# Attention with the values as the stationary operand: what the chip makes of a reordered softmax normalisation

## The reference, cut to what matters

```python
def _window_attention(q, k, v, k_ctx, v_ctx, sink):
    ...
    s_ctx = jnp.einsum('bnqgrd,bcgd->bngrqc', qb, k_ctx).astype(jnp.float32) * scale
    s_sink = jnp.broadcast_to(sink.astype(jnp.float32).reshape(1, 1, g, r, 1, 1), s_win.shape[:-1] + (1,))
    p = jax.nn.softmax(jnp.concatenate([s_win, s_ctx, s_sink], axis=-1), axis=-1).astype(v.dtype)
    o = (jnp.einsum('bngrqk,bnkgd->bnqgrd', p[..., :kw_len], vw)
         + jnp.einsum('bngrqc,bcgd->bnqgrd', p[..., kw_len:-1], v_ctx))
    return o.reshape(b, n, hq * d)
```

## Time and profile before

| | |
|---|---|
| median of three runs | 1915.06 us (1911.14 to 1921.12) |
| profiled execution | 1919.19 us, span 1917.4 us |
| mean granted TensorE clock | 0.982 |
| busy: TensorE, VectorE, ScalarE, GpSimd | 95%, 70%, 55%, 6% |
| attention and start of the output projection, layer 0 | 166 to 282 us |
| the same in layer 1 | 780 to 848 us |

### The profile page before, as it was taken

One profiled execution on the slowest core, in us unless ns is written; L12 is line 12 of the kernel. 1 busy time (PEld: TensorE's weight loads), 2 busy tenths in 40 slices (PEclk: granted clock), 3 DMA queues, 4 the chain that ended last, 5 costly groups with the idle time before them and its releaser, 6 DMA issues.

```text
span 1917.4 us, 23772 instructions
## 1 busy us (share of the span) xinstructions
PE 1822.6 (95%) x8964; PEld 1480.7 (77%) x8964; DVE 1339.3 (70%) x1280; ACT 1050.9 (55%) x1009; POOL 119.9 (6%) x126
## 2 busy tenths in 40 slices
PE   4999899999999999987999999999999999999996
PEld 2986578888888888576888788888888888888885
DVE  2579645333323367756888888889888898898886
ACT  3334644322222153545777776777776776777774
POOL 1123600000000012400000000000000000000000
PEclk8999989999999999997999999999999999999999
DMA  8325823532342234735999999999999999999994
GB/s 291 126 88 207 303 75 78 140 96 86 95 109 83 74 97 132 258 138 175 370 332 354 358 340 345 368 346 354 369 328 362 351 361 359 338 354 352 353 367 154
DMA packets 245911, 472.85 MB, mean 247 GB/s; under 512 B 10546, under 2 KB 60564, under 8 KB 245804
## 3 DMA queue, kind: packets, MB, share of 16 engines
q1 hardware_dynamic: 241712, 468.14, 68.9%
q10 hardware_dynamic: 4092, 3.20, 0.6%
HBM read 470.26 MB, written 1.05 MB: 246 GB/s over the span
## 4 chain that ended last, share of the span: by engine, by line
PE 48%; DMA 21%; DVE 16%; ACT 8%; issue 5%; POOL 2%; SPq 0%; DVEq 0%; ACTq 0%; POOLq 0%
PE bank L543 13%; PE bank L545 13%; PE bank L544 13%; DMA raw<-in_moe_w_gate_dram 10%; DVE parts L1707 9%; ACT parts L1409 6%; DMA raw<-in_moe_w_down_dram 5%; DMA raw<-in_moe_w_up_dram 4%; DMA raw<-in_ada_w_dram 2%; PE bank L561 1%; PE bank L1047 1%; POOL gb L1663 1%; DVE parts L1692 1%; PE bank L790 1%; DVE ACC L2180 1%
## 5 line engine op out<-in xcount | busy, mean ns | idle before, releaser
L1707 DVE TENSOR_TENSOR parts<-raw,parts 128x2048 fp32r<-128x2048 f32 x336 | 764.9, 2289 | 115.0 <-ACT parts L1409 113.9
L1409 ACT ACTIVATE parts<-raw 128x2048 fp32r<-128x2048 f32 x336 | 642.7, 1919 | 260.4 <-DMA raw<-in_moe_w_up_dram 94.9
L543 PE MATMUL bank<-parts,XEr 128*128 128x512 f32 x896 | 357.2, 399 | 8.7 <-DVE parts L1707 6.3
L545 PE MATMUL bank<-parts,XEr 128*128 128x512 f32 x896 | 350.1, 391 | 0.0
L544 PE MATMUL bank<-parts,XEr 128*128 128x512 f32 x896 | 349.4, 390 | 0.0
L1270 ACT ACTIVATE parts<-raw 128x2048 fp32r<-128x2048 f32 (+1 forms) x62 | 113.2, 1831 | 270.2 <-PE bank L545 250.0
L1692 DVE TENSOR_TENSOR parts<-raw,parts 128x2048 fp32r<-128x2048 f32 (+1 forms) x62 | 135.8, 2194 | 138.2 <-ACT parts L1270 137.9
L543 PEld LDWEIGHTS bank<-parts,XEr 128*128 128x128 f32 x896 | 168.7, 188 | 49.9 <-DVE parts L1707 10.3
L545 PEld LDWEIGHTS bank<-parts,XEr 128*128 128x128 f32 x896 | 168.5, 188 | 36.6
L544 PEld LDWEIGHTS bank<-parts,XEr 128*128 128x128 f32 x896 | 168.9, 188 | 32.6
L543 PE MATMUL bank<-parts,HTr 128*128 128x512 f32 x448 | 175.6, 392 | 1.3 <-DVE HTr L1707 0.8
(11 more groups left out here) (245 smaller groups left out, 2289.7 us busy)
## 6 DMA issues: line engine op xcount, KB each, us to landing
raw<-in_moe_w_gate_dram SPq DMA_DIRECT2D x112, 1024.0 KB, 7.2
raw<-in_moe_w_up_dram SPq DMA_DIRECT2D x112, 1024.0 KB, 7.2
raw<-in_moe_w_down_dram SPq DMA_DIRECT2D x112, 1024.0 KB, 6.7
raw<-in_ada_w_dram SPq DMA_DIRECT2D x28, 1024.0 KB, 8.0
more<-in_ada_w_dram SPq DMA_DIRECT2D x20, 1024.0 KB, 7.7
raw<-in_w_in_dram SPq DMA_DIRECT2D x12, 1024.0 KB, 5.1
raw<-in_ffn_w_gate_dram SPq DMA_DIRECT2D x22, 512.0 KB, 4.0
raw<-in_ffn_w_up_dram SPq DMA_DIRECT2D x22, 512.0 KB, 5.4
```

The lines of the kernel that those rows point to most:

```text
L543: nc.tensor.matmul(out, st[0], mv[0], start=start, stop=False)
L545: return nc.tensor.matmul(out, st[1], mv[0], start=False, stop=stop)
L1409: nc.scalar.activation(parts[:, n % PARTS, 0, :], raw[:, r, :], ACT.Copy).then_inc(hi_ready, 1)
L1707: return nc.vector.tensor_tensor(out, a, b, op)
```

## The change

It turns the values product round: a group's 64 value columns are stationary, the transposed probabilities move, and the result comes out as 64 features by 128 queries, group 0 in the lower half of the partitions and group 1 in the upper half, with the blocks of both groups issued alternately. The attended tile is thus already in the layout that the output projection needs, and `turn_attended` is gone. The row sums, which lie one per query and partition, have to be spread over the feature partitions: TensorE multiplies each inverted sum, broadcast to 64 columns, with the identity (`spread_sums`), in two column halves too, into a bank of `AB`; ScalarE copies it to `proj` (`sums_out`); VectorE multiplies `OB` by it (`normalise`). High and low part are then made from `proj`, not from a bank.

The order moves with it. VectorE inverts a tile's sums in the next tile's first step (before: second), TensorE spreads them at the head of the second step, VectorE normalises at the head of the third. For a layer's last tile the inversion comes ahead of the splitting of the output weights. In the third step of a tile TensorE makes its modulation products ahead of the values products. The rows of `w_out` for the attended features are loaded in the new order of features, in two pieces of 64 partitions.

```diff
+        def evacuated(layer, i):
+
+            return layer * (NT + 1) + i + 2
...
             for h in range(2):
-                for k0, k1 in HALVES:
-                    split_item([cols(io["w_out"][layer], h * SLICE, (h + 1) * SLICE, k0, k1)],
-                               k1 - k0, SLICE, n % 2, (n + layer) % 2)
-                    n += 1
+                w = io["w_out"][layer][:, h * SLICE:(h + 1) * SLICE]
+                groups = [w[256 * g:256 * g + 256, :].rearrange("(r p) n -> p r n", p=HEAD_DIM) for g in range(KV_HEADS)]
+                split_item(groups, KT // 2, SLICE, n % 2, (n + layer) % 2)
+                n += 1
+                split_item([cols(w, 0, SLICE, KT // 2, KT)], KT // 2, SLICE, n % 2, (n + layer) % 2)
+                n += 1
...
-            def turn_attended(layer, t):
-
-                b = open_mix(layer, t, 0)
-                for i in range(4):
-                    c = C_Q + i * P
-                    mm = nc.tensor.transpose(b[:, i * P:(i + 1) * P], proj[:, t, c:c + P], ident)
+            def spread_sums(layer, i):
+
+                t = order_of(layer)[i]
+                mixed[layer, t, 0] = len(mixed) + 1
+                b = open_a(("sums", layer, t))
+                after(recip_ready)
+                turn = i % 2
+                for r in range(4):
+                    for g in range(KV_HEADS):
+                        head = g * 4 + r
+                        mm = nc.tensor.matmul(b[64 * g:64 * g + 64, r * P:(r + 1) * P],
+                                              rsum[:, turn, head:head + 1].broadcast_to([P, HEAD_DIM]), ident, start=True, stop=True)
                 mm.then_inc(a_full, 1)
...
-                def values(n):
-                    t, r, g = its[n]
-                    head = g * 4 + r
-                    if n % 8 == 0 and n:
+                def values(m):
+                    t, r, _ = its[2 * m]
+                    if m % 4 == 0 and m:
                         after(att_read)
-                    pe.wait_ge(a_done, job[("probs", layer, n)] + 1)
                     first = 0 if t < TT else TT
+                    pe.wait_ge(a_done, job[("probs", layer, 2 * m + 1)] + 1)
                     for kb in range(first, NT):
-                        mm = nc.tensor.matmul(OB[:, head * 64:(head + 1) * 64], PT[:, n % 4, kb * P:(kb + 1) * P],
-                                              proj[:, kb, C_V + 64 * g:C_V + 64 * g + 64],
-                                              start=(kb == first), stop=(kb == NT - 1))
-                    mm.then_inc(att_done, 1)
+                        for g in range(KV_HEADS):
+                            mm = nc.tensor.matmul(OB[64 * g:64 * g + 64, r * P:(r + 1) * P], proj[:, kb, C_V + 64 * g:C_V + 64 * g + 64],
+                                                  PT[:, (2 * m + g) % 4, kb * P:(kb + 1) * P],
+                                                  start=(kb == first), stop=(kb == NT - 1))
+                            if kb == NT - 1:
+                                mm.then_inc(att_done, 1)
 
                 last = len(its) // 2
                 for m in range(last + 2):
+                    if m % 4 == 1 and m >= 5:
+                        spread_sums(layer, m // 4 - 1)
                     if m < last:
                         scores(2 * m)
                         scores(2 * m + 1)
...
                     if m >= 2:
-                        values(2 * m - 4)
-                        values(2 * m - 3)
-                    if m % 4 == 2 and 6 <= m < last:
-                        turn_attended(layer, order_of(layer)[m // 4 - 1])
-                    if m < last:
+                        if m % 4 == 2 and m < last:
+                            for _ in range(ADA_ITEMS[layer][m]):
+                                ada_product()
+                        values(m - 2)
+                    if m < last and m % 4 != 2:
                         for _ in range(ADA_ITEMS[layer][m]):
                             ada_product()
...
                                 if i == 0:
                                     after(att_read)
-                                    turn_attended(layer, tiles[-1])
...
                 for j, src in enumerate(srcs):
+                    if src.shape[0] == HEAD_DIM:
+                        sp.dma_start(dst[j * HEAD_DIM:(j + 1) * HEAD_DIM, :, :], src).then_inc(raw_loaded[s], 16)
+                        continue
...
+            def attended_high(layer, i):
+
+                t = order_of(layer)[i]
+                act.wait_ge(att_read, evacuated(layer, i))
+                nc.scalar.activation(hTr[:, 0, 0:4, t * P:(t + 1) * P],
+                                     proj[:, t, C_Q:C_RQ].rearrange("p (k n) -> p k n", k=4), ACT.Copy).then_inc(mix_hi, 1)
...
+                def sums_out(i):
+                    copy_out(proj[:, order_of(layer)[i], C_Q:C_RQ], take()[:, :])
...
+                    if m % 4 == 1 and m >= 5:
+                        sums_out(m // 4 - 1)
                     if m >= 1:
                         for n in (2 * m - 2, 2 * m - 1):
...
                     if m % 4 == 2 and 6 <= m < last:
-                        mix_high(order_of(layer)[m // 4 - 1], 0)
+                        attended_high(layer, m // 4 - 1)
                     if m == last - 1:
                         split_to(first["out", layer] + 2)
+                sums_out(last // 4 - 1)
...
-                mix_high(order_of(layer)[-1], 0)
+                attended_high(layer, nt - 1)
...
+                def invert_sums(i):
+                    after(esink_ready)
+                    sums = rsum[:, i % 2, :]
+                    step(tt(sums, sums, esink[:, i % 2, :], ALU.add))
+                    nc.vector.reciprocal(sums, sums).then_inc(recip_ready, 1)
+
+                def normalise(i):
+                    tile = order_of(layer)[i]
+                    dve.wait_ge(att_done, base + 8 * i + 8)
+                    dve.wait_ge(a_done, job[("sums", layer, tile)] + 1)
+                    tt(proj[:, tile, C_Q:C_RQ], OB[:, :], proj[:, tile, C_Q:C_RQ], ALU.mult).then_inc(att_read, 1)
...
                 for m in range(last + 2):
+                    if m % 4 == 2 and 6 <= m < last:
+                        normalise(m // 4 - 1)
...
+                        if m % 4 == 0 and m:
+                            invert_sums(m // 4 - 1)
                         if m % 4 == 3:
...
                     if m == last - 1:
+                        invert_sums(last // 4 - 1)
                         split_to(first["out", layer] + 2)
                     if m == last:
                         ada_rows(layer + 1)
-                    if m % 4 == 1 and m >= 5:
-                        turn = (m // 4 - 1) % 2
-                        tile = order_of(layer)[m // 4 - 1]
-                        after(esink_ready)
-                        step(tt(rsum[:, turn, :], rsum[:, turn, :], esink[:, turn, :], ALU.add))
-                        step(nc.vector.reciprocal(rsum[:, turn, :], rsum[:, turn, :]))
-                        dve.wait_ge(att_done, base + 2 * m - 2)
-                        tt(proj[:, tile, C_Q:C_RQ].rearrange("p (h d) -> p h d", d=HEAD_DIM), OB[:, :].rearrange("p (h d) -> p h d", d=HEAD_DIM),
-                           per_group(rsum[:, turn, :], HEAD_DIM), ALU.mult).then_inc(att_read, 1)
+                    if m == last + 1:
+                        normalise(last // 4 - 1)
...
             def mix_low(layer, t, half):
-                b = a_bank[full[("mix", layer, t, half)]]
+                b = a_bank[full[("mix", layer, t, half)]] if half else proj[:, t, C_Q:C_RQ]
```

More of the change, by code:

```diff
@@ L319, in build @@
         sarg_ready, esink_ready = sem("sink_arg_ready"), sem("sink_exp_ready")
+        recip_ready = sem("row_sums_inverted")
         att_done, att_read = sem("attention_products"), sem("attention_evacuated")
@@ L2030, in attention @@
                         ada_rows(layer + 1)
[L2031 to L2039 removed]
+                    if m == last + 1:
+                        normalise(last // 4 - 1)
                 assert next(rest, None) is None and next(norm, None) is None
             def mix_low(layer, t, half):
[L2043 removed]
+                b = a_bank[full[("mix", layer, t, half)]] if half else proj[:, t, C_Q:C_RQ]
                 k, tok = slice(4 * half, 4 * half + 4), slice(t * P, (t + 1) * P)
                 dve.wait_ge(mix_hi, mixed[layer, t, half])
[L2046 removed]
+                tt(hTr[:, 1, k, tok], (b[:, :] if half else b).rearrange("p (k n) -> p k n", k=4), hTr_f[:, 0, k, tok], ALU.subtract)\
                     .then_inc(mix_lo, 1)
```

1 line of the change is left out of this document (removed).

## The result

The changed kernel took 1922.1 us (median of 20 runs, 1915.5 to 1928.1), the kernel before 1914.95 (20 runs beside them): ratio 1.0029, 95% interval 1.0017 to 1.0041, so 5.5 us, or 0.3%, **slower** (the ratio uses all the runs; the two medians alone lie 7.2 us apart). Forecast was 4.3 us faster. A second series gave 1.0023 (1.0004 to 1.0042). The profiled execution took 1922.04 us, span 1920.2.

What follows compares the result with a forecast made beforehand. TensorE, busy 95% of the span, was taken as the bound where others wait for it. Layer 0's 2.9 us and layer 1's 1.4 sum to 4.3 us, median 1910.8 us; range 1905.5 to 1924.6 us, 82%.

Steps and rivals of the forecast that it cites:

- a gain of 2.9 us: Layer 0's attention: shorter values, removed transposes and earlier output projection, less the sums' spreading, save 2.9 us.
- a gain of 1.4: Layer 1's attention: 1.0 us from steps 5 and 6, 0.44 from the last transposes, 1.4 us together.
- rivals A and B: Values products: A, halves do not overlap, 1919.6 us, 8%; B, loads wait for the running pass, 1914.7 us, 10%.
- The removed wait: Layer 0, step 8: transposes no longer wait for VectorE's low part, 0.85 us earlier, mostly lost at step 9's mask pass.
- The low part reads SBUF rather than a bank, same shape: 0.: VectorE's low part of the attended tile: reading SBUF instead of a bank costs nothing, 0 us.
- and an addition: VectorE, steps 4, 8, 12: an 8-column addition moves there with the reciprocal (0.20 us); step 9's mask pass no earlier, counted 0.
- Both are ready by then ...: 0: VectorE's normalising product heading steps 6, 10, 14: values and ScalarE's sums are ready, so its wait costs 0.
- If half the partitions took twice the time, 2.7 us more is still under the 4.3 us of cover. 0.: Output-weight loads in 64-partition pieces, layer 1: slower landing stays covered, cost 0, up to 2 us if cover is gone.
- Same work ... : 0: Steps 10 and 14, layer 1's step 6: modulation products ahead of values, two loads issued 1 to 2 us earlier, 0.
- rival C: Steps 10 to 13: modulation-weight transfers become the bound, 1.9 us less gain, 1912.7 us, chance 17%.
- Rival D's "opposite": Clock around both layers' output projections: instead of returning sooner (1905.5 us, 12%), it costs as much, 1915 us; no own chance.
- only the second counts after: Layer 0's output projection, behind last values and row copy before, waits only for the row copy afterwards: 0.35 us.

Runs made afterwards that it cites:

- four edits: Changed kernel with whole output-weight loads, sums copy ahead of exponentials, first low part in step 11, layer 1's step 6 values first: ratios to before 0.999, 0.998.
- run 6: Changed kernel with the low part of layer 0's first tile moved from step 7 to step 11: ratio to the kernel before 1.0015.
- run 3: Changed kernel with output weights loaded whole into all 128 partitions, steps pairing other heads: ratio to the kernel before 1.0005.
- run 4: Changed kernel with whole loads and, in layer 1, the values of step 6 ahead of the modulation product again: ratio to the kernel before 1.0003.
- run 9: Four edits plus early row copy, with unused extra matmuls in layer 1's steps, in gaps ending both layers' attention, or both: ratios to before 0.997, 0.9985, 1.002.
- run 1: Kernel before, with the first output-weight item of each column half loaded as two 64-partition transfers: ratio to the kernel before 1.0017.

## Why the prediction was wrong

The failed steps are terms that the prediction put at nothing. In layer 0 it had a gain of 2.9 us and 0.28 us were lost (L0), because VectorE and ScalarE came late in steps 8 to 10. In layer 1 it had a gain of 1.4 and 3.5 to 5.5 were lost (L1), and the largest term there is the loads into 64 partitions, which held up the last modulation weights.

**Right.** Values 1.02 us (forecast 1.00), sums 1.02, a step with new values 5.55 us (forecast about 5.4): the column halves overlap, rivals A and B fall. The rule from the Trainium skill's page "TensorE: Matmul & The Clock Gate", Part 3, that a weight load overlaps running matmuls only if its row groups differ, gave an estimate of 1.43 in the prediction; the trace disagrees. The removed wait came too: the transposes of step 8 start 3.0 us after the mask pass of step 7, before 3.7. The price of the whole, 4.3 us forecast and about 4 found, agrees by luck in part: it was found only with four edits and with the row copy out of the way, and none of these five was in the forecast.

**"The low part reads SBUF rather than a bank, same shape: 0."** This step failed first. While GpSimd works, the subtraction takes 1.75 us; with GpSimd idle 0.68 or less. It has two SBUF operands now. So has, in both kernels, the two-column step behind each mask pass: 1.19 us at 210.89, 0.16 at 231.29 in run 6 with GpSimd done, whereas the mask pass, with one operand in a bank, takes 0.69 in both. This is what the Trainium skill says (page "SBUF — State Buffer", section "SBUF: two separate sides"): VectorE's operations with two SBUF inputs and GpSimd's that read SBUF hold a shared pair of ports by turns, for a whole instruction. Worth 0.91 us of L0 (run 6).

**The reciprocal "and an addition" moved into step 8.** I named the queue behind them and counted nothing. They take 0.35 us, and the tap behind them met GpSimd: 1.71 us instead of 0.74. Step 9's mask pass, forecast level, came 2.5 us later, or 2.8 us later if both are counted from step 7's. Run 6 gave back 1.7 of these. The other 1.1 is about what the inversion and the tap, 1.72 us there too, add; no run moved either alone, so their share is not shown.

**"Both are ready by then ...: 0"** for the product at the head of step 10: it waited 2.14 us. I had looked at when TensorE would have the sums ready, not at where ScalarE's copy stands in ScalarE's own order; I had even priced that copy, but only for the copies behind it. With this and the low part mended together L0 is 2.1 us shorter than changed; singly they give 0.48 and 0.91.

**"If half the partitions took twice the time, 2.7 us more is still under the 4.3 us of cover. 0."** The rate was guessed well, 139 to 254 GB/s for 385. The cover was that of the wrong transfer: I asked when the output weights must be there, and not who shares the queue. The last modulation item, issued at 812.96 and still under way when they followed at 818.08, landed at 825.07; in run 3 with the full rate at 823.81. TensorE waits for that one, not for the weights. Against run 3 the changed kernel loses 1.5 us up to the end of the last product, 1.4 from there to the row copy (values at half clock among it) and 3.1 in the projection at half clock: 5.9 in all, the largest term, of which half is the clock's. That is one pair of profiles; the second one of the changed kernel lies 3.9 us above run 3, and level with run 4, which loads whole too. The timed ratios say 4 us or so: 1.0029 and 1.0023 with the pieces, 1.0005 and 1.0003 with whole loads, though their intervals overlap.

**"Same work ... : 0"** for the modulation products ahead of the values: rival C, a bound by the modulation transfers, was meant for layer 0, where the changed kernel has no such wait. It is true of layer 1 at this step, and there the 1.02 us of values stand behind the wait. That this costs time is read from the chain of run 3; run 4 does not show it in time.

**Rival D's "opposite"**, which I left without a chance of its own, came. Less work on TensorE lowered the granted clock: 3.2 to 10 us at half speed in a stretch that had 0 to 1.1, and in the changed kernel the output projection at 0.50 from 840 to 848 us (0.77 before). That the clock follows the work is shown by run 9; what it costs by itself is not separated, since much of the time lies under waits for transfers. How long the projection stays at the low level is the part that stays open (run 1).

The row copy did bound the end, as predicted for both layers ("only the second counts after"): moving it gave the new values 1.3 us more in L0 and 2.7 to 4.7 us in L1.

## What to carry to other kernels

When an operand moves from a bank to SBUF, or an operation past another, price it on its own engine's queue and against GpSimd, not by its shape. When a load changes its form, ask which transfers share the queue with it, and use all 128 partitions. A saving on the busiest engine shows only after the waits beside it have been moved out of the way: look for the copy that comes last and can come first.

## What was not expected of the hardware

Transfers into 64 partitions ran at 139 to 254 GB/s instead of 385 with the busy share as high as ever, so the share alone hides it. Two column halves of 64 stationary by 128 moving columns take 0.064 us a pass (1.02 for 16), against 0.108 for 128 by 64. And the kernels that give TensorE less to do in these stretches were granted some 0.002 less mean clock, and got it back when the gaps were filled.
